# The first two up pairs of each layer as eight plain block products, and where the first additions of the squares go

## The chip, the cores and the metric

One core of one Trainium2 chip runs the kernel. The metric is the time of one launch in device microseconds (us), as a median of several runs; lower is better.

## The reference

Two token groups (512 prompt rows and 64 sample rows) go through two layers of a hybrid encoder with the same weights. What matters here is the second half of a layer:

```python
x = x + mix @ w_out
u = rmsnorm(x, g2) @ w_up                      # 1024 -> 4096
x = x + jnp.square(jax.nn.relu(u)) @ w_down    # 4096 -> 1024
```

Everything is float32. `rmsnorm(x, g)` is x times the reciprocal root of the mean of its squares, times g.

## The kernel before, in words

**Layout.** Features lie on partitions, the 576 tokens (T) along the free axis, as two halves of 288 (HALF). `x` is eight tiles k of 128 x 576. A float32 product is made of three in the reduced type: each operand is split into a high part and a low part (`xh`, `xl`; `w_hi`, `w_lo`), and TensorE adds hi*hi, hi*lo and lo*hi. ScalarE writes high parts (a copy that rounds), VectorE writes low parts (a subtraction).

**Order.** All of it is written out by hand, one program for each engine, tied by counting semaphores; an engine takes its instructions strictly in that order. The feed-forward stage of a layer runs in four groups (GROUPS) of 1024 hidden features. A group has four up pairs `pi` (each two tiles of 128 hidden features), then eight down tiles. Group 0 is written out (`first`), because the rms of x isn't known yet; it is applied after the down products.

**Up pair by seven products.** `up_pair` computes a pair as a 2 x 2 block product with seven instead of eight block products (Winograd's form): 7 x 4 x 3 = 84 matmuls of 288 columns. For that VectorE adds weight blocks (`up_sums`, lines 1330 to 1335, into `s21` and `s34`), ScalarE and VectorE split the sums, the moving side uses sums of activations (`th`, `tl`, made from `tf` and `t2f`), and the PSUM banks are combined afterwards: ScalarE copies bank a out four times as it grows (`snap` 0 to 3, lines 823, 839, 843, 855; 843 copies bank c), VectorE adds (lines 1404, 1424, 1427). The third product of a pair waits for snap 0, the fifth for snap 1, the sixth for snap 2, the seventh for snap 3. Two of the four sums use the upper half of `xh`, `xl` of tiles 0 to 3 or a slot of `w_hi`, `w_lo`, which must be free of earlier products.

**Plain pair.** In group 0 pair 0 is computed plainly (`plain_pair`): two tiles of 8 x 2 x 3 = 48 matmuls on undivided weights, 96 in all. It needs no sums, and its evacuation is relu (`plain_relu`), square and rounding (`plain_rest`) on ScalarE, and the low part (`hid_low`) on VectorE. Meanwhile the sums of pair 1 and of the activations are made (`first_pair` on ScalarE and VectorE).

**Evacuation of a pair by seven products.** `even_tile` on ScalarE waits for line 1427 on VectorE, then does relu, square and rounding; `odd_tile` follows in the next pair, behind snap 0.

**Squares.** In group 0 ScalarE squares the eight tiles of x (`squares(k)`, line 812) and VectorE adds them (`add_square(k)`, line 1350): k = 0 to 2 in pair 1, 3 to 5 in pair 2, 6 and 7 in pair 3. On ScalarE they stand between snap 2 and snap 3. The squares go into two buffers by turns, so `squares(k)` for k >= 3 waits for `add_square(k - 2)`. After pair 3 TensorE sums over partitions (`sum_squares`, line 1544).

**Loads.** SP loads w_up in blocks of 1 MB for a pair into two stage buffers by turns; the block of pair pi is loaded once the low parts of pair pi - 2 are made (`s_uw`).

Of the kernel before, what the change touches and what calls it, by code (L numbers as in the profile page):

```python
# [19 lines left out]
ACT = mybir.ActivationFunctionType  # L20
AX = mybir.AxisListType

P = 128
DM = 1024
KT = DM // P
# [90 lines left out]
def hymba_step(nc, inputs, outs):  # L116
# [4 lines left out]
    with ExitStack() as ctx:  # L121
# [243 lines left out]
        def up_loaded(l, g, pi):  # L365

            r = pi % 2
            return s_ld[r], landed[PAIRS * l + (S_MLP + 1) // 2 + r] + 16 * (4 * g + pi // 2)
# [126 lines left out]
        def _(act):  # L495
# [90 lines left out]
            for l in range(DEPTH):  # L586
# [145 lines left out]
                def up_hi_raw(g, pi):  # L732

                    act.wait_ge(*up_loaded(l, g, pi))
                    A(w_tile(w_hi, slot_m), raw_of(pi)[:, :, 0:P], ACT.Copy).then_inc(s_uh, 1)
# [37 lines left out]

                def plain_hi(i):

                    act.wait_ge(*up_loaded(l, 0, 0))
                    A(w_tile(w_hi, slot_m + i), tile_raw(i), ACT.Copy).then_inc(s_uh, 2)

                def plain_relu(i, free):

                    A(two(mix[:, i, :]), acc[(tile_m + i) % 2], ACT.Relu).then_inc(free, 1)

                def plain_rest(i, free, step):

                    u = UP * l
                    act.wait_ge(free, u + 3)
                    A(mix[:, i, :], mix[:, i, :], ACT.Square).then_inc(step, 2)
                    act.wait_ge(step, 2 * u + 2)
                    A(hid_h[:, i, :], mix[:, i, :], ACT.Copy).then_inc(s_hidh, 1)

                def first_pair():

                    u = UP * l
                    round_sums(l, 6, 2)
                    act.wait_ge(s_pr, 7 * u + 3)
                    act.wait_ge(s_tl, 5 * l + 2)
                    act.wait_ge(s_tf, 7 * (l + 1))
                    plain_relu(0, s_fd)
                    up_hi_raw(0, 1)
                    plain_rest(0, s_fd, s_ev)  # L800
                    act.wait_ge(s_pr, 7 * u + 4)
                    up_hi_s34(u + 1)
                    round_sums(l, 7, 3)
                    A(small[:, 5:6], eps_col, ACT.Copy).then_inc(s_snap, 4)
                    act.wait_ge(s_pr, 7 * u + 7)
                    up_hi_s21(u + 1, 4)

                def squares(k):

# [3 lines left out]

                def group(g, first=False, last=False):
                    if first:
                        first_pair()
                    for pi in range(int(first), 4):
                        u = UP * l + 4 * g + pi
                        bank_a = psum[:, 6 + pi % 2, 0:HALF]

                        act.wait_ge(s_pr, 7 * u + 1)
                        act.wait_ge(s_fd, u + 2)
                        A(snap[:, 0, :], bank_a, ACT.Copy).then_inc(s_snap, 1)
                        up_hi_a22(pi)
                        if first and pi == 1:
                            plain_relu(1, s_fc)
                            plain_rest(1, s_fc, s_od)
                        elif pi:
                            odd_tile(u - 1, pi - 1)

                        act.wait_ge(s_pr, 7 * u + 2)
                        if pi < 3:
                            up_hi_raw(g, pi + 1)
                        else:
                            down_hi(g, 0)

                        act.wait_ge(s_pr, 7 * u + 3)
                        act.wait_ge(s_fc, u + 2)
                        A(snap[:, 1, :], bank_a, ACT.Copy).then_inc(s_snap, 1)  # L839

                        act.wait_ge(s_pr, 7 * u + 4)
                        act.wait_ge(s_c22, u + 1)
                        A(snap[:, 2, :], psum[:, bank_c + pi % 2, 0:HALF], ACT.Copy).then_inc(s_snap, 1)
                        if first and pi < 3:
                            up_hi_s34(u + 1)
                        elif pi < 3:
                            up_hi_s21(u + 1)
                        elif not first:
                            down_hi(g, 1)
                        if first:  # L850
                            for k in range(3 * pi - 3, min(3 * pi, KT)):
                                squares(k)

                        act.wait_ge(s_pr, 7 * u + 5)
                        A(snap[:, 3, :], bank_a, ACT.Copy).then_inc(s_snap, 1)
                        if first or pi < 3:
                            act.wait_ge(s_pr, 7 * u + 6)
                        if first and pi < 3:
                            up_hi_s21(u + 1, 4)
                        elif pi < 3:  # L860
                            up_hi_s34(u + 1)
                        elif first:
                            down_hi(g, 1)
                        even_tile(u, pi)
                    odd_tile(UP * l + 4 * g + 3, 3)
                    if first:

                        act.wait_ge(s_hid, 8 * GROUPS * l + 8)
                        rms_of(2 * l + 1)
                    for i in range(KT):  # L870
                        act.wait_ge(s_tile, tile_m + 8 * g + i + 1)
                        if i < 6:
                            down_hi(g, i + 2)
                        elif last:
                            split(g0 + SLOTS + i - 6)
                        elif i == 6:
                            up_hi_raw(g + 1, 0)
                        else:
                            up_hi_s21(UP * l + 4 * g + 4)
                            up_hi_s34(UP * l + 4 * g + 4)  # L880
                        if last and l < DEPTH - 1:
                            norm_tile(2 * l + 2, i)
                        elif last:
                            act.wait_ge(*x_ready(2 * DEPTH, i))
                            A(xg[:, i, :], x[:, i, :], ACT.Copy, scale=gain(2 * DEPTH, i)).then_inc(s_xg, 1)
# [48 lines left out]
        def _(dve):  # L934
# [99 lines left out]
            for l in range(DEPTH):  # L1034
# [328 lines left out]
                    V.tensor_tensor(w_tile(w_lo, slot_m + i), tile_raw(i), f(w_tile(w_hi, slot_m + i)),  # L1363
                                    ALU.subtract).then_inc(s_uw, 2)

                def first_pair():

                    u = UP * l
                    plain_lo(1)
                    sum_rounded(1, 3, 2, 4)  # L1370
                    dve.wait_ge(s_xn, KT * (l + 1))
                    V.tensor_tensor(tf[:, 2], xn[1][:, :, HALF:T], xn[0][:, :, HALF:T], ALU.subtract).then_inc(s_tf, 1)
                    V.tensor_tensor(tf[:, 3], t2f, xn[1][:, :, 0:HALF], ALU.subtract).then_inc(s_tf, 1)

                    V.memset(small[:, 1:2], 0.0).then_inc(s_fa, 1)
                    V.memset(small[:, 4:5], 0.0).then_inc(s_c22, 1)
                    V.memset(small[:, 6:7], 0.0).then_inc(s_su, 4)
                    dve.wait_ge(s_cno, 16 * 4 * (l + 1))
                    up_sums(0, 1, u + 1, True)
                    up_lo_raw(u + 1, 1)  # L1380
                    up_lo_s34(u + 1, 2)
                    sum_rounded(0, 1)
                    sum_rounded(2, 4)
                    up_lo_s21(u + 1, 3)
                    sum_rounded(3, 5)

                def group(g, first=False, last=False):
                    if first:
                        first_pair()
                    for pi in range(int(first), 4):  # L1390
                        u = UP * l + 4 * g + pi
                        if pi < 3:
                            up_sums(g, pi + 1, u + 1, first)
# [126 lines left out]
        def _(pe):  # L1520
# [83 lines left out]
            for l in range(DEPTH):  # L1604
# [255 lines left out]
                        ins = products(tile_m + i, lhs, k, k == 0, k == KT - 1, hid_h, hid_l)  # L1860
                    ins.then_inc(s_tile, 1)

                def plain_pair():

                    u = UP * l
                    for i in range(2):
                        pe.wait_ge(s_uw, 4 * u + 2 * i + 2)
                        pe.wait_ge(s_evac, tile_m - 1 + i)
                        for k in range(KT):
                            if i == 0:  # L1870
                                pe.wait_ge(s_xl, KT * (2 * l + 1) + k + 1)
                            lhs = lambda w: w[:, (slot_m + i) % 2, k * P:(k + 1) * P]
                            ins = products(tile_m + i, lhs, k, k == 0, k == KT - 1, xh, xl)
                            if i == 1 and k == 3:
                                ins.then_inc(s_pr, 1)
                        ins.then_inc(s_pr, 3)

                plain_pair()
                for pi in range(1, 4):
                    up_pair(0, pi, pi == 1, True)  # L1880
                sum_squares(2 * l + 1)
                for i in range(KT):
                    down_tile(0, i)
# [62 lines left out]
```

## Time and profile before

| | |
|---|---|
| median of three runs | 1374.21 us (1373.27 to 1374.45) |
| profiled execution | 1374.66 us, its span 1372.8 us |
| busy in the span | PE 97%, DVE 67%, ACT 45%, POOL 6% |
| mean granted clock of TensorE | 0.991 |
| first group of layer 0 | plain pair from 301.35, pairs 1 to 3 from 314.15, down tiles from 353.19 us |
| first group of layer 1 | plain pair from 966.89, pairs 1 to 3 from 979.69, sum of squares at 1017.63 us |

PE is TensorE, DVE VectorE, ACT ScalarE, POOL GpSimd, SP the queue that issues the loads. L1802 is line 1802 of the kernel. The end of a matmul in the profile is modelled; consecutive ones overlap.

### The profile page before, as it was taken

The numbers are of one execution on the slowest core, as the hardware profiler recorded it, in microseconds if no ns is written. First come the engines' busy times: TensorE is split into PE (matmuls) and PEld (weight loads), VectorE is DVE, ScalarE is ACT, GpSimd is POOL, SyncE is SP. The second block draws the span as 40 slices with busy tenths as digits, with TensorE's granted clock in tenths as the row PEclk, the third lists the DMA queues.
The fourth block names the chain that finished last, engine by engine and source line by source line (L and its number), as shares of the span: only waits on it lengthen the run. The fifth ranks groups of instructions, "written<-read, shape, count | busy, mean of one in ns | idle before, by whom it ended". The sixth has DMA issues, their size and how long they took to land.

```text
span 1372.8 us, 24727 instructions
## 1 busy us (share of the span) xinstructions
PE 1328.5 (97%) x10071; PEld 1289.8 (94%) x10071; DVE 913.4 (67%) x1436; ACT 613.8 (45%) x1038; POOL 80.2 (6%) x67
## 2 busy tenths in 40 slices
PE   5999999998999999999999999999999999999997
PEld 5999898898999999999999989989999999999996
DVE  5666787679557467376666777866974844846733
ACT  4324324457428247156242333344771641733732
POOL 2000001100000000000510000010000000000033
PEclk8999999999999999999999999999999999999998
DMA  6322120032223223132252221202222232222311
GB/s 197 93 68 62 62 63 31 32 88 83 93 62 123 73 82 122 61 92 92 62 122 68 63 83 42 62 32 71 69 93 83 75 100 82 92 92 62 121 61 69
DMA packets 116167, 109.20 MB, mean 80 GB/s; under 512 B 21932, under 2 KB 110452, under 8 KB 115956
## 3 DMA queue, kind: packets, MB, share of 16 engines
q1 hardware_dynamic: 109888, 104.60, 25.1%
q10 hardware_dynamic: 6196, 3.45, 0.9%
q8 instruction: 57, 0.93, 0.3%
q14 instruction: 26, 0.21, 0.1%
HBM read 104.24 MB, written 3.81 MB: 79 GB/s over the span
## 4 chain that ended last, share of the span: by engine, by line
PE 82%; DVE 6%; issue 6%; ACT 3%; POOL 1%; DMA 1%; SPq 0%; POOLq 0%; ACTq 0%; DVEq 0%
PE psum L1530 55%; PE psum L1802 7%; PE psum L1804 7%; PE psum L1803 7%; DMA stage<-in_w_in 1%; DVE z L1155 1%; PE psum L1640 1%; PE psum L1760 1%; POOL nq L490 1%; PE psum L1671 1%; PE psum L1667 1%; PE psum L1658 0%; PE psum L1660 0%; POOL wsv L486 0%; DVE x L1047 0%
## 5 line engine op out<-in xcount | busy, mean ns | idle before, releaser
L1530 PE MATMUL psum<-hid_h,w_hi 128*128 128x288 f32 x1280 | 278.6, 299 | 3.9 <-issue 3.9
L1530 PE MATMUL psum<-hid_h,w_lo 128*128 128x288 f32 x1280 | 275.5, 297 | 0.0
L1530 PE MATMUL psum<-hid_l,w_hi 128*128 128x288 f32 x1280 | 274.9, 297 | 0.0
L1530 PEld LDWEIGHTS psum<-hid_h,w_hi 128*128 128x128 f32 x1280 | 207.2, 190 | 5.0 <-issue 4.4
L1530 PEld LDWEIGHTS psum<-hid_h,w_lo 128*128 128x128 f32 x1280 | 207.3, 190 | 0.0
L1530 PEld LDWEIGHTS psum<-hid_l,w_hi 128*128 128x128 f32 x1280 | 207.1, 190 | 0.0
L1530 PE MATMUL psum<-xh,w_hi 128*128 128x288 f32 x800 | 178.2, 305 | 7.9 <-ACT x L570 7.9
L1445 DVE TENSOR_TENSOR tmp<-psum,rms 128x576 f32<-128x576 f32 x64 | 48.5, 757 | 193.6 <-PE psum L1530 193.5
L1530 PE MATMUL psum<-xh,w_lo 128*128 128x288 f32 x800 | 172.2, 297 | 0.0
L1530 PE MATMUL psum<-xl,w_hi 128*128 128x288 f32 x800 | 172.0, 297 | 0.0
L751 ACT ACTIVATE w_hi<-stage 128x1024 fp32r<-128x1024 f32 x64 | 67.7, 1058 | 222.5 <-PE psum L1530 219.9
L1530 PEld LDWEIGHTS psum<-xh,w_hi 128*128 128x128 f32 x800 | 128.7, 190 | 18.5 <-issue 17.9
L1530 PEld LDWEIGHTS psum<-xh,w_lo 128*128 128x128 f32 x800 | 129.7, 190 | 0.0
L1530 PEld LDWEIGHTS psum<-xl,w_hi 128*128 128x128 f32 x800 | 129.6, 190 | 0.0
L521 ACT ACTIVATE w_hi<-stage 128x1024 fp32r<-128x1024 f32 x60 | 63.6, 1061 | 115.2 <-PE psum L1530 115.0
L959 DVE TENSOR_TENSOR w_lo<-stage,w_hi 128x1024 fp32r<-128x1024 f32 (+1 forms) x62 | 73.6, 1188 | 17.9 <-ACT w_hi L521 15.1
L1339 DVE TENSOR_TENSOR w_lo<-stage,w_hi 128x1024 fp32r<-128x1024 f32 x64 | 78.0, 1219 | 8.2 <-ACT w_hi L751 8.2
L1802 PE MATMUL psum<-xh,w_hi 128*128 128x288 f32 x264 | 77.7, 294 | 0.0
L1804 PE MATMUL psum<-xh,w_lo 128*128 128x288 f32 x264 | 77.6, 294 | 0.0
L1803 PE MATMUL psum<-xl,w_hi 128*128 128x288 f32 x264 | 77.6, 294 | 0.0
L1344 DVE TENSOR_TENSOR hid_l<-mix,hid_h 128x576 fp32r<-128x576 f32 x64 | 48.2, 753 | 27.1 <-ACT hid_h L760 14.7
L1802 PE MATMUL psum<-th,w_hi 128*128 128x288 f32 x216 | 63.9, 296 | 0.9 <-ACT snap L839 0.9
(314 smaller groups left out, 2569.2 us busy)
## 6 DMA issues: line engine op xcount, KB each, us to landing
stage<-in_w_up SPq DMA_DIRECT2D x32, 1024.0 KB, 5.5
stage<-in_w_down SPq DMA_DIRECT2D x32, 1024.0 KB, 5.0
stage<-in_w_in SPq DMA_DIRECT2D x18, 1024.0 KB, 5.2
stage<-in_w_in SPq DMA_DIRECT2D x16, 256.0 KB, 4.6
stage<-in_w_out SPq DMA_DIRECT2D x8, 512.0 KB, 6.2
stage<-in_w_out SPq DMA_DIRECT2D x4, 1024.0 KB, 5.1
z<-in_x_prompt SPq DMA_DIRECT2D x4, 512.0 KB, 5.9
out<-z SPq DMA_DIRECT2D x4, 512.0 KB, 3.7
```

The lines of the kernel that those rows point to most:

```text
L490: nc.gpsimd.tensor_tensor(nq[0:r, :, 0:r], nq[0:r, :, 0:r], sw[0:r, :, 0:r], ALU.add).then_inc(s_dn, 1)
L521: A(w_hi[:, g % 2, :].rearrange("p (k c) -> p k c", k=k), stage[:, n % 2, :].rearrange("p (k q c) -> p k q c", k=k, q=2)[:, :, (s + 1) % 2 ...
L751: A(w_tile(w_hi, slot_m + i), tile_raw(i), ACT.Copy).then_inc(s_hi, 1)
L959: V.tensor_tensor(pick(w_lo), src, f(pick(w_hi)), ALU.subtract).then_inc(s_lo, 1)
L1155: link(V.reciprocal(zz, zz))
L1339: V.tensor_tensor(w_tile(w_lo, slot_m + i), tile_raw(i), f(w_tile(w_hi, slot_m + i)), ALU.subtract).then_inc(s_lo, 1)
L1344: V.tensor_tensor(hid_l[:, k, :], mix[:, k % 2, :], f(hid_h[:, k, :]), ALU.subtract).then_inc(s_hid, 1)
L1445: V.tensor_tensor(two(tmp[0][:]), acc[(tile_m + i) % 2], two(rms[:]), ALU.mult).then_inc(s_dm, 1)
L1530: ins = M(acc[t % 2][:, a, :], lhs(w), mov[:, k, a * HALF:(a + 1) * HALF], start=first and n == 0, stop=last and n == 2)
L1802: M(out, hi, mh, start=start and k == 0, stop=False, skip_group_check=not start)
L1803: M(out, hi, ml, start=False, stop=False, skip_group_check=not start)
L1804: ins = M(out, lo, mh, start=False, stop=k == 3, skip_group_check=not start)
```

## The change

In group 0 of each layer pairs 0 and 1 are computed plainly, four tiles one behind the other (`plain_tile(i)`); pairs 2 and 3 stay with seven products, and the roles of the first such pair (`first`) go to pair 2. Tiles 2 and 3 use the same two weight slots and PSUM accumulators as tiles 0 and 1 and wait for these. `first_pairs` holds the new order of ScalarE and VectorE. Squares 0 to 2 go from pair 1, where they stood ahead of snap 3, to ScalarE's order between the evacuations of tiles 1 and 2; additions 1 and 2 go to VectorE's order between the sums of pair 2 and its first low part. The place of squares and additions 3 to 7 in pairs 2 and 3 is as it was. Counters that pair 1 used to raise are raised by the larger steps of the memsets and of one small copy.

The diff, cut to its core:

```diff
                 def plain_hi(i):
 
-                    act.wait_ge(*up_loaded(l, 0, 0))
+                    act.wait_ge(*up_loaded(l, 0, i // 2))
+                    if i >= 2:
+                        act.wait_ge(s_pr, 7 * UP * l + (3, 7)[i - 2])
...
-                def first_pair():
+                def first_pairs():
 
                     u = UP * l
                     round_sums(l, 6, 2)
-                    act.wait_ge(s_pr, 7 * u + 3)
                     act.wait_ge(s_tl, 5 * l + 2)
                     act.wait_ge(s_tf, 7 * (l + 1))
                     plain_relu(0, s_fd)
-                    up_hi_raw(0, 1)
+                    plain_hi(2)
                     plain_rest(0, s_fd, s_ev)
-                    act.wait_ge(s_pr, 7 * u + 4)
-                    up_hi_s34(u + 1)
                     round_sums(l, 7, 3)
-                    A(small[:, 5:6], eps_col, ACT.Copy).then_inc(s_snap, 4)
-                    act.wait_ge(s_pr, 7 * u + 7)
-                    up_hi_s21(u + 1, 4)
+                    plain_relu(1, s_fc)
+                    plain_hi(3)
+                    plain_rest(1, s_fc, s_od)
+                    for k in range(3):
+                        squares(k)
+                    plain_relu(2, s_fd)
+                    up_hi_raw(0, 2)
+                    plain_rest(2, s_fd, s_ev)
+                    act.wait_ge(s_pr, 7 * (u + 1) + 4)
+                    up_hi_s34(u + 2)
+                    A(small[:, 5:6], eps_col, ACT.Copy).then_inc(s_snap, 8)
+                    act.wait_ge(s_pr, 7 * (u + 1) + 7)
+                    up_hi_s21(u + 2, 4)
...
-                        if first and pi == 1:
-                            plain_relu(1, s_fc)
-                            plain_rest(1, s_fc, s_od)
+                        if first and pi == 2:
+                            plain_relu(3, s_fc)
+                            plain_rest(3, s_fc, s_od)
                         elif pi:
                             odd_tile(u - 1, pi - 1)
...
+                    sum_rounded(0, 1)
+                    plain_lo(2)
+                    hid_low(0, 0)
+                    sum_rounded(2, 4)
+                    sum_rounded(3, 5)
+                    hid_low(0, 1)
+                    plain_lo(3)
                     dve.wait_ge(s_cno, 16 * 4 * (l + 1))
-                    up_sums(0, 1, u + 1, True)
-                    up_lo_raw(u + 1, 1)
-                    up_lo_s34(u + 1, 2)
-                    sum_rounded(0, 1)
-                    sum_rounded(2, 4)
-                    up_lo_s21(u + 1, 3)
-                    sum_rounded(3, 5)
+                    up_sums(0, 2, u + 2, True)
+                    add_square(1)
+                    add_square(2)
+                    up_lo_raw(u + 2, 2)
+                    up_lo_s34(u + 2, 2)
+                    up_lo_s21(u + 2, 3)
...
-                plain_pair()
-                for pi in range(1, 4):
-                    up_pair(0, pi, pi == 1, True)
+                for i in range(4):
+                    plain_tile(i)
+                for pi in range(2, 4):
+                    up_pair(0, pi, pi == 2, True)
```

## Rows read from the trace of the kernel before

**Rows 1.** Part 1 of the page: busy time, share of the span, instructions.
```profile
PE 1328.5 (97%) x10071; PEld 1289.8 (94%) x10071; DVE 913.4 (67%) x1436; ACT 613.8 (45%) x1038; POOL 80.2 (6%) x67
```

**Rows 2.** Part 4 of the page: the chain that ended last, by engine.
```profile
PE 82%; DVE 6%; issue 6%; ACT 3%; POOL 1%; DMA 1%; SPq 0%; POOLq 0%; ACTq 0%; DVEq 0%
```

**Rows 3.** By stretch: length, busy PE, PEld, DVE, ACT, POOL (instructions), granted clock, DMA share, GB/s.
```profile
301.35:314.15 12.80, 12.80 (x98) 12.80 (x97) 12.15 (x18) 9.65 (x14) 0.00 (x0) 1.00 0.29 84
314.15:326.75 12.60, 11.38 (x86) 11.17 (x85) 12.43 (x16) 9.73 (x17) 0.00 (x0) 1.00 0.22 67
326.75:341.29 14.54, 11.83 (x86) 11.23 (x85) 13.85 (x21) 10.77 (x19) 0.00 (x0) 1.00 0.26 88
341.29:352.44 11.15, 11.15 (x87) 11.15 (x86) 7.23 (x11) 9.28 (x17) 0.00 (x0) 1.00 0.29 96
...
979.69:991.95 12.26, 11.38 (x86) 11.17 (x85) 12.09 (x15) 9.59 (x15) 0.00 (x0) 1.00 0.23 69
991.95:1006.48 14.53, 11.83 (x86) 11.22 (x85) 13.84 (x21) 10.78 (x19) 0.00 (x0) 1.00 0.27 87
```

**Rows 4.** TensorE's waits, 300 to 358 us: total, times, longest.
```profile
PE psum L1802 <- ACT snap L823: 1.5, 1, 1.5
PE psum L1802 <- issue: 1.2, 1, 1.2
PE psum L1802 <- ACT snap L855: 0.8, 1, 0.8
PE psum L1802 <- ACT snap L839: 0.5, 1, 0.5
```

**Rows 5.** TensorE in order of time: start, length, operation, idle before and releaser.
```profile
315.73 0.29 PE L1802 MATMUL psum<-xh,w_hi 128*128 128x288 f32 x1
...
325.08 0.37 PE L1802 MATMUL psum<-th,w_h 128*128 128x288 f32 x1 [1.22 <-issue]
...
339.63 0.37 PE L1802 MATMUL psum<-th,w_h 128*128 128x288 f32 x1 [0.78 <-ACT snap L855]
```

**Rows 6.** ScalarE in order of time, layer 0 and one row of layer 1.
```profile
309.31 0.65 ACT L781 ACTIVATE mix<-psum 128x576 f32<-128x576 f32 x1 [0.18 <-DVE tf L1373]
309.85 1.05 ACT L735 ACTIVATE w_hi<-stage 128x1024 fp32r<-128x1024 f32 x1
...
328.98 0.69 ACT L756 ACTIVATE mix<-mix 128x576 f32<-128x576 f32 x1 [3.04 <-DVE mix L1427]
...
338.50 0.68 ACT L812 ACTIVATE tmp<-x 128x576 f32<-128x576 f32 x1 [0.82 <-DVE ssum L1350]
339.09 0.39 ACT L855 ACTIVATE snap<-psum 128x288 f32<-128x288 f32 x1
...
340.96 0.69 ACT L756 ACTIVATE mix<-mix 128x576 f32<-128x576 f32 x1 [0.53 <-DVE mix L1427]
...
343.07 0.41 ACT L823 ACTIVATE snap<-psum 128x288 f32<-128x288 f32 x1
...
979.88 1.06 ACT L739 ACTIVATE w_hi<-s 128x1024 fp32r<-128x1024 f32 x1 [0.41 <-PE psum L1530]
```

**Rows 7.** VectorE in order of time, layer 0.
```profile
324.32 1.22 DVE L1303 TENSOR_TENSOR w_lo<-stage,w_hi 128x1024 fp32r<-128x1024 f32 x1
...
326.59 0.75 DVE L1350 TENSOR_TENSOR ssum<-ssum,tmp 128x576 f32<-128x576 f32 x1
...
328.86 1.22 DVE L1308 TENSOR_TENSOR w_lo<-s,w_hi 128x1024 fp32r<-128x1024 f32 x1
330.18 0.69 DVE L1330 TENSOR_TENSOR s<-stage 128x512 f32<-128x512 f32 x1
...
335.24 1.22 DVE L1303 TENSOR_TENSOR w_lo<-stage,w_hi 128x1024 fp32r<-128x1024 f32 x1
...
337.72 0.75 DVE L1350 TENSOR_TENSOR ssum<-ssum,tmp 128x576 f32<-128x576 f32 x1
```

**Rows 8.** Part 6 of the page: loads, KB each, us from issue to landing.
```profile
stage<-in_w_up SPq DMA_DIRECT2D x32, 1024.0 KB, 5.5
```

More of the change, by code:

```diff
@@ L774, in plain_hi @@
                 def plain_hi(i):
-                    act.wait_ge(*up_loaded(l, 0, 0))
+                    act.wait_ge(*up_loaded(l, 0, i // 2))
+                    if i >= 2:
+                        act.wait_ge(s_pr, 7 * UP * l + (3, 7)[i - 2])
                     A(w_tile(w_hi, slot_m + i), tile_raw(i), ACT.Copy).then_inc(s_uh, 2)
                 def plain_relu(i, free):
-                    A(two(mix[:, i, :]), acc[(tile_m + i) % 2], ACT.Relu).then_inc(free, 1)
+                    if i >= 2:
+                        act.wait_ge(s_hid, 8 * GROUPS * l + i - 1)
+                    act.wait_ge(s_pr, 7 * (UP * l + i // 2) + (3, 7)[i % 2])
+                    A(two(mix[:, i % 2, :]), acc[(tile_m + i) % 2], ACT.Relu).then_inc(free, 1)
                 def plain_rest(i, free, step):
-                    u = UP * l
+                    u = UP * l + i // 2
                     act.wait_ge(free, u + 3)
-                    A(mix[:, i, :], mix[:, i, :], ACT.Square).then_inc(step, 2)
+                    A(mix[:, i % 2, :], mix[:, i % 2, :], ACT.Square).then_inc(step, 2)
                     act.wait_ge(step, 2 * u + 2)
-                    A(hid_h[:, i, :], mix[:, i, :], ACT.Copy).then_inc(s_hidh, 1)
-                def first_pair():
+                    A(hid_h[:, i, :], mix[:, i % 2, :], ACT.Copy).then_inc(s_hidh, 1)
+                def first_pairs():
                     u = UP * l
                     round_sums(l, 6, 2)
-                    act.wait_ge(s_pr, 7 * u + 3)
                     act.wait_ge(s_tl, 5 * l + 2)
@@ L815, in group @@
                     if first:
-                        first_pair()
-                    for pi in range(int(first), 4):
+                        first_pairs()
+                    for pi in range(2 if first else 0, 4):
                         u = UP * l + 4 * g + pi
@@ L1364, in plain_lo, with first_pairs @@
                                     ALU.subtract).then_inc(s_uw, 2)
-                def first_pair():
+                def first_pairs():
                     u = UP * l
@@ L1373, in first_pair @@
                     V.tensor_tensor(tf[:, 3], t2f, xn[1][:, :, 0:HALF], ALU.subtract).then_inc(s_tf, 1)
-                    V.memset(small[:, 1:2], 0.0).then_inc(s_fa, 1)
-                    V.memset(small[:, 4:5], 0.0).then_inc(s_c22, 1)
-                    V.memset(small[:, 6:7], 0.0).then_inc(s_su, 4)
-                    dve.wait_ge(s_cno, 16 * 4 * (l + 1))
-                    up_sums(0, 1, u + 1, True)
-                    up_lo_raw(u + 1, 1)
-                    up_lo_s34(u + 1, 2)
-                    sum_rounded(0, 1)
-                    sum_rounded(2, 4)
-                    up_lo_s21(u + 1, 3)
-                    sum_rounded(3, 5)
+                    V.memset(small[:, 1:2], 0.0).then_inc(s_fa, 2)
+                    V.memset(small[:, 4:5], 0.0).then_inc(s_c22, 2)
+                    V.memset(small[:, 6:7], 0.0).then_inc(s_su, 8)
+                    sum_rounded(0, 1)
[5 more added lines that the diff above has]
+                    plain_lo(3)
+                    dve.wait_ge(s_cno, 16 * 4 * (l + 1))
+                    up_sums(0, 2, u + 2, True)
[4 more added lines that the diff above has]
+                    up_lo_s21(u + 2, 3)
                 def group(g, first=False, last=False):
                     if first:
-                        first_pair()
-                    for pi in range(int(first), 4):
+                        first_pairs()
+                    for pi in range(2 if first else 0, 4):
                         u = UP * l + 4 * g + pi
@@ L1861, in down_tile, with plain_tile @@
                     ins.then_inc(s_tile, 1)
[L1863 to L1867, printed above, removed]
+                def plain_tile(i):
+                    pe.wait_ge(s_uw, 4 * UP * l + 2 * i + 2)
+                    if i < 2:
                         pe.wait_ge(s_evac, tile_m - 1 + i)
[L1869 to L1876, printed above, removed]
-                plain_pair()
-                for pi in range(1, 4):
-                    up_pair(0, pi, pi == 1, True)
+                    else:
+                        pe.wait_ge((s_fd, s_fc)[i - 2], UP * l + 3)
+                    for k in range(KT):
+                        if i == 0:
+                            pe.wait_ge(s_xl, KT * (2 * l + 1) + k + 1)
+                        lhs = lambda w: w[:, (slot_m + i) % 2, k * P:(k + 1) * P]
+                        ins = products(tile_m + i, lhs, k, k == 0, k == KT - 1, xh, xl)
+                        if i % 2 and k == 3:
+                            ins.then_inc(s_pr, 1)
+                    ins.then_inc(s_pr, 3)
+                for i in range(4):
+                    plain_tile(i)
+                for pi in range(2, 4):
+                    up_pair(0, pi, pi == 2, True)
                 sum_squares(2 * l + 1)
```

## The prediction

> **What bounds the kernel now.** I read the page first: TensorE is busy 97% of the span [rows 1] and its work makes 82% of the chain that ended last [rows 2]. A busy share says little about where TensorE waits, so the second view is the table by stretch, cut at the start of each up pair of the first group. The plain pair takes 12.80 us. Of the three pairs by seven products behind it the last takes 11.15, the other two 12.60 and 14.54 in layer 0, 12.26 and 14.53 in layer 1 [rows 3]. The layer 1 stretches that are not printed (966.89 to 979.69 and 1006.48 to 1017.63) are 12.80 and 11.15 again. So a pair costs 11.15 where nothing waits, and the first group loses 1.45 + 3.39 = 4.84 us in layer 0 and 1.11 + 3.38 = 4.49 in layer 1. Nothing else in the stage waits. The third view, TensorE's waits, names the places: one in the first such pair and three in the second, all released by a copy out of PSUM on ScalarE (the one called "issue" starts right behind the copy of line 855) [rows 4]. These idle times add up to only 4.0 us, since the profile's matmul is 0.29 us long while the next one starts 0.13 us after it (12.80 by 96) [rows 3, 5]; I therefore go by starts, and by the stretches.
>
> The Trainium skill says the same of every trace (Perfetto Trace Analysis, the summary of the profiler window): the end of a TensorE instruction is an estimate. Here the idle rows would give 3.9 us to win in layer 0 and the starts give 4.84; the starts decide.
>
> The fourth view is the order in time of ScalarE and VectorE, to see what is late behind those copies [rows 6, 7]. VectorE is busy 12.43 of 12.60 and 13.85 of 14.54 us in the two slow pairs [rows 3]: it forms the four sums of weight blocks, the low parts, and adds the squares, in a fixed order.
>
> **What the change adds on TensorE.** A plain pair is 12.80 us against 11.15, so 1.65 us in each layer, 3.3 us in all, and this lies on the path: nothing covers it.
>
> **Is plain pair 1 fed in time?** I write the schedule of layer 0; tile 2 is due at 314.15, tile 3 at 320.55, pair 2 at T0 = 326.95.
> - Tile 2. ScalarE evacuates tile 0 at 309.31 and starts the weight copy 0.54 later, as it does today for another weight [rows 6]; the high part is there at 310.9. VectorE's low part takes 1.22 [rows 7], so 312.1, 2.0 early. Its load was issued before the stage; a load lands 5.5 us after issue [rows 8].
> - Tile 3. ScalarE gets tile 1's end 0.19 us after the next stretch begins (979.88 against 979.69) [rows 3, 6]: 314.34. Then 0.54 for the evacuation, 1.06 for the high part, 0.69 each for square and copy: 317.3. VectorE's low part of tile 3 is queued behind hid_low(0, 1), which waits for that copy; 0.75 and 1.22 make 319.3, 1.25 early. Behind that new wait stand all sums of pair 2, and SP's load of pair 3, which is issued at 319.3, some 3 us earlier than today.
> - Pair 2's weights. VectorE: four sums (2.6), two additions of squares (0.86 each), one low part (1.22) from 319.3: 324.8. The high part comes at 320.55 + 0.19 + 0.54 + 1.05 = 322.3. First product due 326.95: 2.1 early. The half of xh that takes two sums is free at half of tile 3 (323.95), high and low by 326.3; it is due at T0 + 3.2.
>
> So pair 1's 1.45 (1.11) us is gone, and the additions 1 and 2 of squares, moved ahead, cost nothing: VectorE idles before T0 anyway. If that cover were gone they would cost 1.7 us a layer. The memsets and the extra semaphore steps are 0.06 us each, hidden.
>
> **Is pair 2 fed in time?** It is now the first with seven products. The wait of its third product (1.5 idle, on the copy of line 823) came from ScalarE standing 3.04 us on VectorE for the even tile of pair 1 [rows 4, 6]. That tile no longer exists; ScalarE takes the copy 1.78 us after the pair's start, as it does in pair 3 today (343.07 against 341.29) [rows 3, 6]. So this wait and that of line 839 behind it go. What is late next is the seventh product. It needs snap 3, which stands on ScalarE behind squares 3, 4 and 5, and square 5 waits for addition 3 on VectorE, since its buffer is square 3's. The diff leaves this order as it is in pi = 2. From T0:
> - ScalarE rounds the sum in tile 3's slot at 0.19 (it waits for tile 3's end), 1.06 long, and VectorE starts its low part at 1.28.
> - The four sums of pair 3 start 1.32 later (328.86 to 330.18): 2.60.
> - From them to the low part of the next raw block is 5.06 (330.18 to 335.24): 7.66.
> - Two low parts to the first addition: 2.27 (324.32 to 326.59). Pair 2 of today shows 2.48, but there ScalarE was late for the second; I take 2.27. Addition 3 starts at 9.93 [rows 7].
> - Square 5 starts 0.78 later (337.72 to 338.50), snap 3 0.59 later, the seventh product 0.54 later (339.09 to 339.63): 11.84 [rows 5 to 7]. Six products of 1.59 (11.15 by seven) would have had it due at 9.54. It waits 2.3 us.
> - From there to the next pair is 1.66 (339.63 to 341.29) [rows 3, 5]: pair 2 takes 13.50.
>
> Pair 3 keeps its 11.15: the even tile's relu starts 3.24 after addition 3 (337.72 to 340.96), at 13.17, 0.33 before pair 3, exactly as today [rows 3, 6, 7].
>
> **Sum.** Layer 0: 12.80 + 13.50 + 11.15 = 37.45 against 12.60 + 14.54 + 11.15 = 38.29, so -0.84. Layer 1: 37.45 against 37.94, so -0.49. Together -1.3 us. Everything behind is bound by TensorE and shifts whole. The profiled execution took 1374.66 us, 1.86 more than its span of 1372.8, and 0.45 more than the median of the runs, 1374.21. The sum gives 1373.3 for a profiled execution and **1372.9 us** for the median. Bounds: each 0.1 us on VectorE's row of work before addition 3 is worth 0.2 us. Taking 2.48 for 2.27 gives 1373.3; if TensorE got pair 2 without its wait, 1368.3.
>
> One rule of the skill weighs on that row of work. The rows show that an operation which waits for the one before it on VectorE starts later than a free one: 1.32 us behind a low part instead of 1.13 (two low parts and an addition behind each other) [rows 7]. The Trainium skill (VectorE: DVE Perf Modes, The DRAIN you can't avoid) says that a semaphore between Vector operations costs nothing extra. By it the row would be shorter by about 0.2 us at this place and the kernel by 0.4; the row decides.
>
> **Rivals.**
> - *The seventh product does not wait* (chance 0.12; by more than 0.7 us a layer less than I say). VectorE would have to come to addition 3 by T0 + 7.6. Against it: the row of work is fixed, and an earlier snap 3 alone wins nothing, since pair 3's first copy stands behind the even tile, which hangs on the same additions, and its third product would wait instead. For it: VectorE starts the row without today's backlog. If it is all true: 1372.9 - 4.6 = 1368.3 us.
> - *Slower: pair 3 takes over the waits of pair 2* (0.08). Place: the even tile of pair 2 on ScalarE, behind which the first snap of pair 3 is queued. Price: what pair 2 pays today without its last wait (0.8 idle, 1.0 by starts), 3.39 less 1.0 = 2.4 us a layer, so 1372.9 + 4.8 = 1377.7. It decides when that relu starts over 0.8 us later against pair 3 than it does now: the copy ends 2.2 us into pair 3 and is due at 3.2. For it: ScalarE stood 3.04 us at this very place in the pair that was first behind the plain one [rows 6]. Against it: there the seventh product left early, 1.4 us late only, while here it is itself held by the additions.
> - *Tile 3 late* (0.04). VectorE's low part comes over 1.25 us later than worked out, say 1 us beyond: 1374.9.
>
> **Chances.** The forecast has 0.76, with a range of its own from 1371.5 to 1374.3 (0.5 us of VectorE's row either way and 0.6 us of spread in the runs). Reaching to both sides for the rest: 1370.5 to 1374.9. A measurement of this kernel tells about 0.2% (2.7 us) from no change, so faster means below 1371.5, slower above 1376.9. Faster 0.12, same 0.80, slower 0.08.
>
> **What would show it.** In the trace after, both plain pairs take 12.80 us with no wait; pair 2 has one wait, at its seventh product, about 2.1 us idle, released by the copy of the fourth snap; no wait at its third and fifth; pair 3 takes 11.15; ones-matmuls of the squares start 37.45 us after tile 2. Wrong would be: a wait ahead of tile 2, tile 3 or pair 2 (VectorE's new order), a wait in pair 3 (the slower rival), or a pair 2 near 11.2 us.

## The result, and the profile after

The changed kernel takes 1377.08 us (median of 20 runs, 1373.93 to 1378.98), the kernel before 1374.55 us (20 runs, 1371.75 to 1378.41). The ratio is 1.0017, with a 95% interval of 1.0009 to 1.0025: slower by 1.2 to 3.4 us, where 1.3 us less had been forecast. The profiled execution took 1377.53 us, its span 1375.3, and TensorE's mean granted clock in it is 0.987 (0.991 before). The two profiled spans differ by 2.5 us: 1.75 of it lies in the two stages of the change, 0.57 ahead of layer 0's stage (it starts at 301.92 instead of 301.35), in work that the change doesn't touch.

First the table by stretch of the changed kernel, cut as [rows 3]: four plain tiles in two stretches, then pairs 2 and 3; above for layer 0, below for layer 1. The stretch comes first; the columns are length, busy time of PE, PEld, DVE, ACT and POOL with instructions, granted clock, share of the DMA engines, GB/s.

```profile
301.92:314.72 12.80, 12.80 (x98) 12.80 (x97) 11.98 (x17) 8.76 (x12) 0.00 (x0) 1.00 0.28 84
314.72:327.52 12.80, 12.80 (x98) 12.80 (x97) 9.61 (x12) 8.59 (x13) 0.00 (x0) 1.00 0.28 82
327.52:341.51 13.99, 11.88 (x86) 11.67 (x85) 12.22 (x17) 10.33 (x17) 0.00 (x0) 0.96 0.23 76
341.51:353.72 12.21, 12.21 (x86) 12.21 (x85) 6.78 (x11) 8.86 (x16) 0.00 (x0) 0.91 0.26 87
...
993.76:1008.24 14.48, 12.37 (x87) 12.17 (x86) 12.54 (x17) 10.83 (x17) 0.00 (x0) 0.92 0.22 74
1008.24:1019.94 11.70, 11.70 (x86) 11.70 (x86) 6.46 (x10) 8.36 (x16) 0.00 (x0) 0.95 0.28 90
```

The two plain pairs are as forecast, 12.80 us each and without a wait. The two pairs behind them take 26.20 and 26.18 us, where 24.65 was forecast, and the new thing is in the clock column: it is below 1.00 there, in both layers, where [rows 3] have 1.00 throughout. Pair 3 is longer than 11.15 although TensorE is busy in all of it.

TensorE in order of time shows the place, in layer 0:

```profile
339.35 0.38 PE L1820 MATMUL psum<-th,w_h 128*128 128x288 f32 x1 [2.11 <-issue]
339.56 0.30 PE L1821 MATMUL psum<-tl,w_h 128*128 128x288 f32 x1
...
340.23 0.29 PE L1820 MATMUL psum<-th,w_h 128*128 128x288 f32 x1
340.36 0.39 PE L1821 MATMUL psum<-tl,w_h 128*128 128x288 f32 x1
340.55 0.44 PE L1822 MATMUL psum<-th,w_l 128*128 128x288 f32 x1
340.79 0.44 PE L1820 MATMUL psum<-th,w_h 128*128 128x288 f32 x1
...
343.43 0.44 PE L1822 MATMUL psum<-xh,w_lo 128*128 128x288 f32 x1
343.67 0.37 PE L1820 MATMUL psum<-xh,w_hi 128*128 128x288 f32 x1
343.88 0.29 PE L1821 MATMUL psum<-xl,w_hi 128*128 128x288 f32 x1
```

It waits once, 2.11 us, at the seventh product of pair 2, which is the wait that was forecast, and starts it 11.83 us after the pair began (339.35 less 327.52). One microsecond later (340.36) matmuls start every 0.24 us instead of every 0.13, for 3.3 us (340.36 to 343.67). That is the lower of the two clock levels, 1.2 GHz; the 14 matmuls in it cost 0.107 us more each, 1.5 us. In layer 1 the table at 2 us a stretch shows the same behind the wait that ends at 1005.58:

```profile
1004.16:1006.16 2.00, 0.58 (x4) 0.61 (x5) 1.79 (x4) 1.66 (x3) 0.00 (x0) 0.96 0.01 4
1006.16:1008.16 2.00, 2.00 (x10) 2.00 (x10) 1.90 (x4) 1.44 (x3) 0.00 (x0) 0.50 0.03 8
1008.16:1010.16 2.00, 2.00 (x13) 2.00 (x12) 0.00 (x0) 0.88 (x2) 0.00 (x0) 0.69 0.00 0
1010.16:1012.16 2.00, 2.00 (x17) 2.00 (x16) 0.64 (x2) 1.56 (x4) 0.00 (x0) 1.00 0.00 0
```

Why TensorE waited is read from ScalarE and VectorE of layer 0, the rows that answer to [rows 6] and [rows 7]:

```profile
327.72 1.06 ACT L739 ACTIVATE w_hi<-s 128x1024 fp32r<-128x1024 f32 x1 [2.05 <-PE psum L1548]
...
338.27 0.68 ACT L824 ACTIVATE tmp<-x 128x576 f32<-128x576 f32 x1 [1.68 <-DVE ssum L1362]
338.86 0.39 ACT L867 ACTIVATE snap<-psum 128x288 f32<-128x288 f32 x1
```

```profile
328.81 1.23 DVE L1320 TENSOR_TENSOR w_lo<-s,w_hi 128x1024 fp32r<-128x1024 f32 x1 [1.97 <-ACT w_hi L739]
330.14 0.69 DVE L1342 TENSOR_TENSOR s<-stage 128x512 f32<-128x512 f32 x1
...
335.21 1.22 DVE L1315 TENSOR_TENSOR w_lo<-stage,w_hi 128x1024 fp32r<-128x1024 f32 x1
336.35 1.22 DVE L1325 TENSOR_TENSOR xl<-s,xh 128x1024 fp32r<-128x1024 f32 x1
337.48 0.75 DVE L1362 TENSOR_TENSOR ssum<-ssum,tmp 128x576 f32<-128x576 f32 x1
```

Square 5 (338.27) waits 1.68 us for addition 3 (337.48), and snap 3 (338.86) behind it releases the seventh product at 339.35. The trace's "issue" at that product is this copy, as in [rows 4].

### The profile page after: what moved, and what is told of

Same layout as the page of the kernel before. It is cut to its first block, busy times and chain, and to the rows that moved or that the text cites. A ratio compares the mean times of both kernels' runs of the same rounds, so it can differ in the third digit from the quotient of the medians.

```text
span 1375.3 us, 24733 instructions
## 1 busy us (share of the span) xinstructions
PE 1334.4 (97%) x10095; PEld 1296.6 (94%) x10095; DVE 903.5 (66%) x1418; ACT 608.2 (44%) x1024; POOL 80.3 (6%) x67
## 4 chain that ended last, share of the span: by engine, by line
PE 87%; issue 5%; DVE 3%; ACT 1%; DMA 1%; POOL 1%; SPq 0%; POOLq 0%; DVEq 0%; ACTq 0%
PE psum L1548 59%; PE psum L1820 7%; PE psum L1822 7%; PE psum L1821 7%; DMA stage<-in_w_in 1%; DVE z L1167 1%; PE psum L1658 1%; PE psum L1778 1%; POOL nq L490 1%; PE psum L1689 1%; PE psum L1685 1%; PE psum L1676 0%; PE psum L1678 0%; POOL wsv L486 0%; PE psum L1562 0%
## 5 line engine op out<-in xcount | busy, mean ns | idle before, releaser
L1548 PE MATMUL psum<-xh,w_hi 128*128 128x288 f32 x864 | 191.9, 304 | 8.5 <-ACT x L570 8.5
L1548 PE MATMUL psum<-xh,w_lo 128*128 128x288 f32 x864 | 185.7, 297 | 0.0
L1548 PE MATMUL psum<-xl,w_hi 128*128 128x288 f32 x864 | 185.5, 296 | 0.0
L1548 PEld LDWEIGHTS psum<-xh,w_hi 128*128 128x128 f32 x864 | 138.9, 190 | 19.1 <-issue 18.5
L1548 PEld LDWEIGHTS psum<-xl,w_hi 128*128 128x128 f32 x864 | 139.8, 190 | 0.0
L1548 PEld LDWEIGHTS psum<-xh,w_lo 128*128 128x128 f32 x864 | 139.8, 189 | 0.0
L1820 PE MATMUL psum<-xh,w_hi 128*128 128x288 f32 x240 | 71.4, 297 | 0.0
L1821 PE MATMUL psum<-xl,w_hi 128*128 128x288 f32 x240 | 71.2, 297 | 0.0
L1822 PE MATMUL psum<-xh,w_lo 128*128 128x288 f32 x240 | 71.1, 296 | 0.0
```

The lines of the kernel that those rows point to most:

```text
L1548: ins = M(acc[t % 2][:, a, :], lhs(w), mov[:, k, a * HALF:(a + 1) * HALF], start=first and n == 0, stop=last and n == 2)
L1820: M(out, hi, mh, start=start and k == 0, stop=False, skip_group_check=not start)
L1821: M(out, hi, ml, start=False, stop=False, skip_group_check=not start)
L1822: ins = M(out, lo, mh, start=False, stop=k == 3, skip_group_check=not start)
```

## The experiments

The experiments were timed in three sets of runs, each on one chip with the kernel before beside the others. A profiled execution also gives the length of the stage, from the first matmul of tile 0 to the ones-matmul of the squares; it repeats to 0.02 us from one profiled execution to the next (the changed kernel: 51.80 and 51.78 in layers 0 and 1, then 51.79 and 51.78), while whole times spread by several us. So the verdicts rest on the stage and the clock in it, with the times beside them.

| kernel | stage, layer 0 / 1, us | longest idle in it, us | half clock in it | median (runs) | ratio to before, 95% |
|---|---|---|---|---|---|
| before | 51.09 / 50.74 | 1.47 / 1.45 | no | 1374.55 (20) | |
| changed | 51.80 / 51.78 | 2.11 / 2.11 | both | 1377.08 (20) | 1.0009 to 1.0025 |
| changed, again | 51.79 / 51.78 | 2.11 / 2.12 | both | 1377.78 (12) | 0.9997 to 1.0019 |
| square 5 behind snap 3 | 50.14 / 50.14 | 1.31 / 1.32 | no | 1373.94 (12) | 0.9972 to 0.9992 |
| squares spread | 47.88 / 47.90 | none | no | 1367.82 (6) | 0.9925 to 0.9951 |
| squares spread, again | 47.90 / 47.89 | none | no | 1370.43 (10) | 0.9952 to 0.9976 |
| squares back | 50.49 / 50.49 | 0.97 / 0.98 | no | 1374.64 (12) | 0.9985 to 1.0011 |
| spread, 3 extra copies | 49.20 / 49.20 | 1.07 / 1.07 | no | 1372.01 (10) | 0.9969 to 0.9992 |
| spread, 5 extra copies | 51.64 / 51.63 | 1.96 / 1.96 | both | 1376.67 (10) | 0.9998 to 1.0021 |
| spread, 8 extra copies | 52.88 / 52.76 | 3.29 / 3.29 | both | 1379.65 (5) | 1.0033 to 1.0064 |
| one plain pair, squares later | 50.37 / 50.01 | 1.51 / 1.51 | no | 1374.06 (12) | 0.9990 to 1.0010 |

"Half clock" is the lower of the two clock levels. The kernel before had medians of 1376.23, 1375.06 and 1374.58 us in the three sets. The columns of stage, idle and clock come from one profiled execution in each row, with two stages in it.

**Is the half clock there every time?** The changed kernel again.

> The changed kernel itself, beside the others on one chip. Theory (the long wait of TensorE ahead of pair 2's seventh product, 2.1 us idle, is followed by 3.4 us at half clock, worth 1.5 us in each layer): 2 to 3 us over the kernel before, and a granted clock of about 0.50 over 3.4 us right behind that wait in both layers. Rival (the half clock came by chance in the one profiled execution): no fall here in one or both layers, and then about 1.3 us under the kernel before.

Half clock in both layers once more. The timed runs say it too, for each comes with its mean granted clock: 0.9889 and 0.9883 on average over the 20 and 12 runs of the changed kernel, 0.9909 and 0.9907 over the 29 and 27 runs of the kernel before in two of the sets. Two stretches of 3.4 us at half clock lower the mean by 2 x 1.7 / 1375 = 0.0025. The difference is 0.0020 to 0.0026, so on average most of these falls are there. It doesn't show them in every execution: 5 of the 32 runs have a mean of 0.991, as with two falls fewer, and took 1373.93 to 1375.99 us. A mean doesn't tell which falls are missing; they can be those of other stretches.

**The wait cut in two.** The changed kernel, square 5 moved on ScalarE.

```diff
-                            for k in range(3 * pi - 3, min(3 * pi, KT)):
+                            for k in range(3 * pi - 3, 5 if pi == 2 else KT):
                                 squares(k)
...
                         A(snap[:, 3, :], bank_a, ACT.Copy).then_inc(s_snap, 1)
+                        if first and pi == 2:
+                            squares(5)
```

> The changed kernel with one order changed: ScalarE takes square 5 behind snap 3 of pair 2 instead of ahead of it. VectorE's order is untouched. The long wait is cut into two short ones: no wait at pair 2's seventh product, instead about 1.6 us at pair 3's third product (its snap 0 stands behind the even tile, which hangs on the same additions) and about 0.7 us at its fifth. The sum of waits is the same as in the changed kernel. Theory (clock): no half clock in this stage, 12.8 + 24.7 us for plain pair 1 to pair 3, 3 us faster than the changed kernel, 1.3 us faster than before. Rival (only the sum of waits counts): the same time as the changed kernel.

Its table by stretch (the plain pairs together, pair 2, pair 3) and TensorE's waits in layer 0:

```profile
303.17:328.77 25.60, 25.60 (x194) 25.60 (x193) 21.60 (x27) 17.34 (x25) 0.00 (x0) 1.00 0.28 83
328.77:339.92 11.15, 11.15 (x87) 11.15 (x86) 9.48 (x13) 8.36 (x14) 0.00 (x0) 1.00 0.28 96
339.92:353.31 13.39, 11.63 (x87) 11.23 (x86) 9.47 (x15) 10.62 (x19) 0.00 (x0) 1.00 0.24 80
```

```profile
PE psum L1822 <- ACT snap L835: 1.3, 1, 1.3
PE psum L1822 <- ACT snap L851: 0.5, 1, 0.5
```

Nothing of VectorE's work is less, and TensorE still waits over 2 us by starts (13.39 less 11.15 is 2.24). The stage is 1.66 us shorter than in the changed kernel in layer 0, 1.64 in layer 1, and the clock column is 1.00. The two short waits cost their own length (24.54 is 2.24 over two pairs of 11.15), the long one cost 1.6 us on top. Pairs 2 and 3 together take 24.54 us, 0.1 less than the 24.65 that the prediction had worked out for the changed kernel: its sum holds where the clock stays up. The median is 3.8 us under the changed kernel's of the same set, where 3 had been expected.

**How long a wait.** The spread kernel (below), in which TensorE never waits, with ScalarE held up ahead of snap 3 of pair 2 by 3, 5 and 8 extra copies of the same bank; the edit with five:

```diff
+                        if first and pi == 2:
+                            for _ in range(5):
+                                link(A(snap[:, 3, :], bank_a, ACT.Copy))
                         A(snap[:, 3, :], bank_a, ACT.Copy).then_inc(s_snap, 1)
```

> The spread kernel with ScalarE held up ahead of snap 3 of pair 2 by three extra copies of the same bank, each waiting for the one before (0.43 us each): TensorE should wait about 1.2 us (1.0 idle) at the seventh product of pair 2, in both layers, and nowhere else. Theory (a short wait costs its own length, a long one brings the clock down): 1.2 us a layer over the spread kernel, clock 1.00 in the stage. Rival (any wait there brings it down): 2.8 us a layer.

> The same with five extra copies: a wait of about 2.2 us, 2.1 idle, the size of the one in the changed kernel, at the same product. Theory (the length of the wait decides): half clock for 3.4 us behind it, 2.2 + 1.5 us a layer over the spread kernel. Rival (the clock falls because of the work around the wait, not its length): clock stays 1.00, 2.2 us a layer.

> The same with eight extra copies: a wait of about 3.5 us. Theory: one stretch of half clock of the same 3.4 us, beginning during the wait or behind it, so 3.5 us plus up to 1.5 us a layer over the spread kernel; the fall is a fixed price and doesn't grow with the wait. Rival (the price grows with the wait): over 3.5 + 2.5 us a layer.

In layer 0 the seventh product starts 10.79, 11.68 and 13.01 us after its pair, and 9.54 is due: waits of 1.25, 2.14 and 3.47 us. The stage is longer than the spread kernel's 47.9 by 1.30, 3.74 and 4.98. So what comes on top of the wait is nothing, 1.6 and 1.5 us (1.4 in layer 1 with eight copies). The price is there or not, and it doesn't grow from the middle wait to the long one. The wait of 1.96 us idle (five copies) and the table at 2 us a stretch behind it:

```profile
339.88 0.37 PE L1829 MATMUL psum<-th,w_h 128*128 128x288 f32 x1 [1.96 <-issue]
```

```profile
339.88:341.88 2.00, 2.00 (x13) 2.00 (x14) 1.88 (x3) 1.97 (x3) 0.00 (x0) 0.85 0.00 0
341.88:343.88 2.00, 2.00 (x10) 2.00 (x9) 1.53 (x3) 0.88 (x2) 0.00 (x0) 0.50 0.00 0
343.88:345.88 2.00, 2.00 (x15) 2.00 (x14) 0.05 (x1) 1.01 (x3) 0.00 (x0) 0.80 0.00 0
```

Here VectorE and ScalarE do other things around the wait than in the changed kernel, and TensorE does the same products as in the spread kernel, which has no wait and keeps its clock. So the wait is the cause and not the work next to it.

With eight copies the clock falls before TensorE starts again: it is down to a mean of 0.84 in a stretch in which TensorE does nothing, while the seventh product starts at 341.92 (and in layer 1 at 1007.75, with 0.83 in 1007.20 to 1007.40).

```profile
341.60:341.80 0.20, 0.00 (x0) 0.00 (x0) 0.00 (x0) 0.20 (x2) 0.00 (x0) 0.84 0.00 0
```

In the eight places the fall starts from 0.4 us ahead of the end of the wait to 1.4 us behind it. No run kept a wait's length and moved it in time, so whether its place in time also decides is open.

**No wait at all: the version that beats both.** Squares and additions go where the two engines idle.

```diff
                     A(small[:, 5:6], eps_col, ACT.Copy).then_inc(s_snap, 8)
+                    squares(3)
+                    squares(4)
...
-                            for k in range(3 * pi - 3, min(3 * pi, KT)):
+                            for k in ((5, 6) if pi == 2 else (7,)):
                                 squares(k)
...
                     up_lo_s34(u + 2, 2)
+                    add_square(3)
+                    add_square(4)
...
+                        if first and pi == 3:
+                            add_square(5)
+                            add_square(6)
                         up_lo_a22(u, pi)
...
-                        if first:
-                            for k in range(max(3 * pi - 3, 1), min(3 * pi, KT)):
-                                add_square(k)
+                        if first and pi == 3:
+                            add_square(7)
```

> The changed kernel with the squares spread: squares and additions 3 and 4 join the plain pair 1 (ScalarE and VectorE idle about 2 us each there), squares 5 and 6 stay in pair 2 with no addition on VectorE, additions 5 and 6 go to VectorE's idle time at the start of pair 3, square and addition 7 stay. Theory: no wait of TensorE is left in pairs 2 and 3; 12.80 + 11.15 + 11.15 = 35.1 us against 39.0 of the changed kernel and 38.3 and 37.9 before: 6 us under before, 1368 us or so. Rival (VectorE bounds pair 2 anyway by its sums and low parts): pair 2 stays over 12 us and the gain is under 3 us.

> The kernel with the squares spread again, as the base of the three with a delay. 1368 us or a little under it, 8 us under before; no wait of TensorE and no half clock in the two stages.

```profile
299.64:312.44 12.80, 12.80 (x98) 12.80 (x97) 11.98 (x17) 8.75 (x12) 0.00 (x0) 1.00 0.28 84
312.44:325.24 12.80, 12.80 (x98) 12.80 (x97) 10.27 (x13) 9.74 (x15) 0.00 (x0) 1.00 0.27 82
325.24:336.39 11.15, 11.15 (x87) 11.15 (x86) 10.28 (x15) 9.36 (x15) 0.00 (x0) 1.00 0.29 96
336.39:347.52 11.13, 11.13 (x86) 11.13 (x85) 8.13 (x12) 8.68 (x16) 0.00 (x0) 1.00 0.30 96
```

The stage is 3.2 and 2.8 us shorter than before, 6.0 in all, and 3.9 us a layer shorter than in the changed kernel. The two intervals together reach from 0.9925 to 0.9976, and 1 less 6.0 / 1375 = 0.9956 lies in the second and just above the first. VectorE is busy 10.28 of 11.15 us in pair 2, where the changed kernel has 12.22 of 13.99: the rival, that its sums and low parts bound the pair anyway, falls. The second run was expected at 1368 us, 8 us under the kernel before; it came out at 1370.43, 4.6 under, and its profiled execution has half clock from about 31, 276 and 939 us on, outside the stage; the first had none at these three.

**The early squares taken back.** Two plain pairs, but no square during them. Squares 0 to 2 go to pair 2, and squares 3 to 5 go from there to pair 3, so this is not the plain half of the change alone:

```diff
-                    for k in range(3):
-                        squares(k)
...
-                            for k in range(3 * pi - 3, min(3 * pi, KT)):
+                            for k in (range(3) if pi == 2 else range(3, KT)):
                                 squares(k)
...
-                    add_square(1)
-                    add_square(2)
...
-                            for k in range(max(3 * pi - 3, 1), min(3 * pi, KT)):
+                            for k in ((1, 2) if pi == 2 else range(3, KT)):
                                 add_square(k)
```

> The changed kernel without its second half: two plain pairs, but no square or addition during them; squares 0 to 2 and additions 1 and 2 in pair 2, the rest in pair 3. Theory: squares 0 to 2 need no addition, so pair 2's seventh product waits about 0.6 us only and pair 3's under 1 us, no half clock, pairs 2 and 3 about 24.4 us together, 1.8 us a layer less than the changed kernel: the moving of the first additions was then worth nothing by itself. Rival (the move brings the gain): slower than the changed kernel by the 1.7 us of two additions in each layer.

The stage is 1.3 us a layer shorter than the changed kernel's: three short waits (0.32, 0.45 and 0.97 idle) and no half clock. Pairs 2 and 3 take 24.9 us, 0.5 over the expectation. The early squares were not the trouble. What they are worth by themselves this run doesn't separate, since the later ones moved too; without half clock it comes to 0.35 us more than square 5 behind snap 3 (24.89 against 24.54). What brings the long wait is square 5 with its own wait ahead of snap 3 of pair 2.

And one plain pair with the squares later, in the kernel before:

```diff
-                        if first:
-                            for k in range(3 * pi - 3, min(3 * pi, KT)):
+                        if first and pi > 1:
+                            for k in ((0, 1, 2) if pi == 2 else range(3, KT)):
                                 squares(k)
...
+                        if first and pi == 3:
+                            add_square(1)
+                            add_square(2)
                         up_lo_a22(u, pi)
...
-                        if first:
-                            for k in range(max(3 * pi - 3, 1), min(3 * pi, KT)):
+                        if first and pi == 3:
+                            for k in range(3, KT):
                                 add_square(k)
```

> The kernel before, one plain pair, with the squares later: none in pair 1, squares 0 to 2 in pair 2 without an addition, additions 1 and 2 in VectorE's idle time at the start of pair 3, squares and additions 3 to 7 behind them in pair 3. It asks whether the second plain pair is needed for the gain of the spread kernel or only the room it gives the additions. Theory (pair 1 is held by VectorE's backlog, not by the additions alone): pair 1 without its wait at the seventh product, 11.15 us; pair 2 still waits about 1.5 us at its third product and 0.6 at its fifth; pair 3 about 1 us at its seventh: 36.6 us for the three against 38.3 before, so 1.7 us a layer faster than before, but slower than the spread kernel by 1 us a layer or more. Rival (the additions are the whole trouble): 33.5 us for the three, faster than the spread kernel.

Pair 1 lost its wait, pair 2 waits 0.98 and 0.46 us idle, and pair 3 waits 1.51 at its seventh product, half a microsecond more than the 1 us expected. The stage is 0.72 and 0.73 us shorter than before, less than half of the 1.7 expected, and the times don't tell it from the kernel before. With one plain pair I found no room for the additions that costs nothing; a better order may exist and wasn't tried.

## Why the prediction was wrong

- *What bounds the kernel, and the price of a plain pair*: right. 12.80 against 11.15 us; both plain pairs came out at 12.80.
- *Is plain pair 1 fed in time?* Right. No wait ahead of tile 2, tile 3 or pair 2. VectorE waited 1.78 us for the copy of tile 1 that the prediction named, and the low part of tile 3 still ended at 319.74, before the tile was due (321.12).
- *Is pair 2 fed in time?* Right to 0.02 us up to the seventh product: 11.83 us after the pair's start (11.82 in layer 1) against 11.84, 2.11 us idle against about 2.1. The waits behind lines 823 and 839 went. The prediction took this wait for the last cost of the pair, and from there on it is wrong.
- *The step that failed* is the next one: "From there to the next pair is 1.66", and pair 3 "keeps its 11.15". They measured 2.16 and 12.21 us in layer 0, 2.66 and 11.70 in layer 1. The 1.66 and 11.15 that it used come from pairs behind waits of 1.5 us and less, where the clock stayed at its upper level. So the time that a wait costs beyond its length was put at nothing, from rows that couldn't show it. Behind this longer wait the clock fell to the lower one for 3.4 us, worth 1.55 us in layer 0 (26.20 less 24.65) and 1.53 in layer 1. The sum of the stages turns from -0.84 and -0.49 into +0.71 and +1.04: +1.75 us for -1.3. This lies in the interval of the measured ratio, 1.2 to 3.4 us.
- *The trace of before had shown it.* The prediction read its clock only in the stage, where it is 1.00. The same trace has a wait of nearly the same length elsewhere, 27 us ahead of the stage, and what followed it. TensorE first, then the clock around it:

```profile
274.19 0.50 PE L1530 MATMUL psum<-hid_h,w_hi 128*128 128x288 f32 x2 [1.97 <-issue]
```

```profile
270.00:275.00 5.00, 2.89 (x22) 2.66 (x23) 3.04 (x8) 2.62 (x5) 0.00 (x0) 1.00 0.00 0
275.00:280.00 5.00, 5.00 (x28) 5.00 (x27) 3.22 (x5) 0.00 (x0) 0.00 (x0) 0.66 0.60 144
```

  A mean of 0.66 over 5 us is 3.4 us at half clock (1 less 0.5 x 3.4 / 5). Layer 1 has the same wait at 939.72 and 0.66 in 940 to 945. A forecast that leaves a wait of 2.3 us should have set this row beside it, and given "the clock falls" as a rival at +1.75 us, 1376.0.
- *The rivals.* None of the three came about: there was a wait at the seventh product, pair 3 had none, tile 3 was in time. The argument against the first rival, that an earlier snap 3 alone wins nothing because pair 3 waits instead, proved right for the waits (square 5 behind snap 3) and wrong for the time, since two short waits are cheaper than one long one.
- *The range* ended at 1374.9, and the measured 1377.08 lies above it. Its upper end left out any cost that a wait has beyond its length, and it took 0.6 us of spread from three runs, where 20 runs reach from 1371.75 to 1378.41.
- *The sentence of the Trainium skill on Vector semaphores* (VectorE: DVE Perf Modes, The DRAIN you can't avoid) was put aside for the row, and the row was right: addition 3 started 9.96 us after the pair (337.48 less 327.52), 9.93 worked out, and the first sum, which waits for the low part ahead of it, started 1.33 us behind it (328.81 to 330.14), a free low part 1.14 (335.21 to 336.35).

## What to carry to other kernels

In this kernel a wait of TensorE had two prices: its length, and the time at half clock around its end if it was about 2 us or more. So when a change gathers several short waits into one, look in the trace for waits of that length anywhere, read the granted clock behind each, and add that to the sum, or give it as a rival where the waits disagree. If the wait can't be removed, try to split it: two waits of 1.3 and 0.5 us, 3.9 us apart, did better here than one of 2.1. How close together two may stand isn't shown. And ask of each instruction that is moved not only whether it fits in its new place but whether the ones left behind still stand in the queue ahead of something that releases TensorE: here the same second plain pair with the later squares moved too took 6 us off the two stages, where the change as it was added 1.75.

## What the runs showed of the hardware

- Half clock came with every idle stretch of TensorE in this stage of 1.96 us and more (8 of 8: two layers in two profiled executions of the changed kernel, and with five and eight extra copies), and with none of 1.51 us and less. Each time it lasted about 3.4 us and cost 1.4 to 1.6 us, for a wait of 1.96 as for one of 3.29. These are four executions, and nothing between 1.51 and 1.96 was tried.
- A wait of 1.97 us elsewhere doesn't bring it each time. Every kernel here has the wait of 1.96 to 1.98 us that the trace of before shows ahead of the stage, once in each layer; over the eleven profiled executions half clock follows it in 15 of 22 places. The first execution of the spread kernel kept the clock:

```profile
273.99 0.51 PE L1554 MATMUL psum<-hid_h,w_hi 128*128 128x288 f32 x2 [1.97 <-issue]
```

```profile
275.00:280.00 5.00, 5.00 (x40) 5.00 (x39) 3.02 (x5) 0.00 (x0) 0.00 (x0) 1.00 0.64 156
```

  What decides there isn't settled by these runs.
- Outside the stage half clock also came without a wait of this length. With three extra copies it starts at 243.0 and 908.6 us, with square 5 behind snap 3 at 908.7, each time behind two short waits close together, here 1.05 and 0.52 us within 2.1 us:

```profile
240.92 1.16 PE L1778 MATMUL psum<-qw,cst 128*128 128x128 f32 x8 [1.05 <-DVE qw L1242]
241.83 0.64 PE L1781 MATMUL psum<-bcr,rconst 128*128 128x128 f32 x4
243.00 2.08 PE L1787 MATMUL psum<-nq,io 128*128 128x512 f32 x2 [0.52 <-POOL nq L490]
```

```profile
240.00:245.00 5.00, 3.56 (x15) 2.28 (x16) 3.46 (x8) 1.09 (x2) 1.27 (x1) 0.80 0.58 213
```

  So the safe 1.51 us holds for single waits in this dense stage, and no more.
- Stretches at half clock account for much of the spread of whole times: the runs of the kernel before with a mean clock of 0.989 took 1377.7 us on average (13 runs), those with 0.993 took 1372.4 (9 runs), 5.3 us less, where 0.004 of 1375 us is 5.5.
- The Trainium skill (TensorE: Matmul & The Clock Gate, What's actually happening) describes a gate that halves the clock when TensorE has been idle and gives it back when it has been busy. The trace agrees on the two levels (matmul starts 0.24 and 0.13 us apart) and on the return: TensorE was busy in all of the 3.4 us at half clock behind the wait of 1.96 us, and then the clock was at 1.00. How much idling a fall takes, these runs show only as far as the counts above.
